# Expert search, segment pacing and gate rows rearranged in a two-layer hybrid decoder trunk

## The reference

```python
mod = silu(c) @ ada_w[l] + ada_b[l]                    # sh_m, sc_m, g_m, sh_f, sc_f, g_f
x = x + g_m * mixer(modulated_norm(x, sh_m, sc_m))
h = modulated_norm(x, sh_f, sc_f)
q = (h @ wq).reshape(128, 8, 2, 128)                   # 8 heads, two halves, chunks of 128 tokens
s = einsum('thcd,hcnd->thcn', q, subkeys)              # 128 scores for each half
sv, si = top_k(s, 16)
cand = sv[..., 0, :, None] + sv[..., 1, None, :]       # 256 candidates
fv, fpos = top_k(cand, 16)                             # 16 experts of each head: 128 a token
coef = softmax(fv) * gelu(u[eidx] . h)
x = x + g_f * sum(coef * v[eidx])
```

## Time and profile before

| | us |
|---|---|
| median of three runs | 1900.18 |
| lowest, highest | 1897.82, 1906.14 |
| the profiled execution's own time | 1903.03 |
| its span in the trace | 1901.2 |
| PE busy | 1616.6 (85%) |
| DVE busy | 1394.7 (73%) |
| ACT busy | 673.4 (35%) |
| POOL busy | 515.2 (27%) |

### The profile page before, as it was taken

How to read it: one execution, slowest core, us unless ns; L and a number is a source line. 1 busy time by engine, 2 the same in 40 slices (tenths; PEclk the granted TensorE clock), 3 DMA queues, 4 the chain that set the end, 5 groups by cost and what they waited for, 6 DMA issues and landing times.

```text
span 1901.2 us, 20926 instructions
## 1 busy us (share of the span) xinstructions
PE 1616.6 (85%) x6868; PEld 1006.0 (53%) x6868; DVE 1394.7 (73%) x3315; ACT 673.4 (35%) x1640; POOL 515.2 (27%) x564
## 2 busy tenths in 40 slices
PE   1767678898999998898999998898999997887776
PEld 1656665554665655564665655554665652332222
DVE  5866598997856758998765748988765759985554
ACT  1313114334732334335632235325632233331112
POOL 2000013222233232222233232222232233343331
PEclk9889788998999999998999999999999998999999
DMA  9982688997799999998999999998899999999996
GB/s 393 422 346 101 242 353 348 367 421 286 283 399 421 422 420 395 363 422 313 321 403 421 421 421 399 370 402 293 287 403 421 421 415 401 416 407 421 421 421 256
DMA packets 96989, 706.08 MB, mean 371 GB/s; under 512 B 10992, under 2 KB 11504, under 8 KB 13296
## 3 DMA queue, kind: packets, MB, share of 16 engines
q0 software_dynamic: 80640, 587.24, 77.1%
q1 hardware_dynamic: 16240, 117.50, 15.1%
HBM read 703.64 MB, written 1.05 MB: 371 GB/s over the span
## 4 chain that ended last, share of the span: by engine, by line
PE 49%; DVE 28%; DMA 16%; ACT 3%; issue 3%; POOL 0%; DVEq 0%; ACTq 0%; POOLq 0%
PE psum L772 26%; DMA ringmem<-in_peer_uv_dram,eidx 11%; DVE ringmem L1435 9%; PE psum L648 5%; PE psum L412 4%; DMA W<-in_w_groups_dram 3%; PE psum L635 2%; DMA ringmem<-in_ada_pairs_dram 2%; PE psum L520 1%; PE psum L508 1%; DVE ringmem L1079 1%; PE psum L518 1%; PE psum L415 1%; DVE coef L1448 1%; ACT diag L1050 1%
## 5 line engine op out<-in xcount | busy, mean ns | idle before, releaser
L772 PE MATMUL psum<-ringmem,diag 128*128 128x512 f32 x2048 | 978.4, 624 | 132.3 <-ACT diag L1050 132.0
L379 POOL DMA_INDIRECT ringmem<-in_peer_uv_dram,eidx x512 | 489.5, 956 | 1131.5 <-PE psum L772 1079.7
L1435 DVE SCALAR_TENSOR_TENSOR ringmem<-ringmem,psum 128x1024 f32<-128x1024 f32 x512 | 612.5, 1220 | 195.3 <-DMA ringmem<-in_peer_uv_dram,eidx 180.1
L772 PEld LDWEIGHTS psum<-ringmem,diag 128*128 128x128 f32 x2048 | 389.1, 199 | 608.1 <-issue 409.1
L1050 ACT ACTIVATE diag<-K,coef 128x128 f32<-128x128 f32 x512 | 176.4, 393 | 225.8 <-DVE coef L1448 225.6
L412 PE MATMUL psum<-hT,W 128*128 128x128 f32 x1344 | 172.3, 287 | 40.9 <-DMA W<-in_w_groups_dram 19.1
L412 PEld LDWEIGHTS psum<-hT,W 128*128 128x128 f32 x1344 | 169.2, 203 | 64.9 <-issue 38.0
L1042 ACT ACTIVATE coef<-dots 128x2 f32<-128x2 f32 x256 | 51.8, 202 | 408.6 <-DVE ringmem L1435 407.7
L1079 DVE SCALAR_TENSOR_TENSOR ringmem<-ringmem,diag 128x1024 f32<-128x1024 f32 x96 | 115.3, 1223 | 20.9 <-DMA ringmem<-in_ada_pairs_dram 18.8
L648 PEld LDWEIGHTS psum<-hT,W 128*128 128x128 f32 x1024 | 123.2, 197 | 12.8 <-issue 7.2
L648 PE MATMUL psum<-hT,W 128*128 128x128 f32 x1024 | 126.0, 281 | 3.1 <-ACT hT L821 3.0
(11 more groups left out here) (243 smaller groups left out, 1629.7 us busy)
## 6 DMA issues: line engine op xcount, KB each, us to landing
ringmem<-in_ada_pairs_dram POOLq DMA_DIRECT2D x48, 1024.0 KB, 19.0
W<-in_w_pieces_dram SPq DMA_DIRECT2D x48, 1024.0 KB, 9.2
W<-in_w_groups_dram SPq DMA_DIRECT2D x24, 1536.0 KB, 11.3
W<-in_w_groups_dram SPq DMA_DIRECT2D x12, 1024.0 KB, 9.6
ringmem<-in_peer_uv_dram,eidx POOLq DMA_INDIRECT x512, 11.7
W<-in_w_groups_dram SPq DMA_DIRECT2D x4, 1040.0 KB, 9.2
attn<-in_subkeys_t_dram SPq DMA_DIRECT2D x4, 1024.0 KB, 9.5
K<-in_consts_dram SPq DMA_DIRECT2D x1, 1546.0 KB, 18.1
```

The lines of the kernel that those rows point to most:

```text
L379: nc.gpsimd.indirect_dma_start(slot(k), None, rows, bass.IndirectOffsetOnAxis(ap=eidx[:, ph % 2, m:m + 1], axis=0)).then_inc(row_landed[q ...
L772: mm = nc.tensor.matmul(acc[:, q], diag[:, k % DIAGS, :], slot(k)[:, D:][:, q], start=(k % SEL == 0), stop=(k % SEL == SEL - 1), skip_grou ...
L1435: ins = v.scalar_tensor_tensor(out=u, in0=u, scalar=1.0, in1=hrep, op0=ALU.mult, op1=ALU.mult, accum_out=dots[:, j:j + 1])
```

## The change

Four things are changed.

The search: from unit 1 on, heads 0 to 3 are searched beside the queries, in segments 61 to 76. In the pass, two heads are searched in ticks 1 to 4, two parts a tick, and heads 6 and 7 in ticks 13 to 20, one part a tick. Unit 0 has only heads 0 and 1 searched in the lead; in its pass heads 4 and 5 stand in ticks 5 to 12.

The pacing: fourteen segments whose work waits on the segment before (1, 2, 43 to 51, 55 to 57) come at most one to a tick; segments start in tick 0 rather than 1; the costs of the last five segments are others. The result: segments 0, 1 and 2 stand in ticks 0, 1 and 2 (before: all in tick 1); segments 5 to 36 each stand about one tick earlier, segment 22 in tick 15 (before: 16), 23 and 24 in 16 (before: 17), 29 in 19 (before: 20), 33 in 23 (before: 24); segments 46 and 47 stand in ticks 37 and 38 (before: both in 38); from segment 48 on they stand where they stood or up to a tick off; 69 to 76 fill ticks 56 to 61.

The gate rows: PE turns the column itself, read as a 128x128 operand with a step of zero, and ACT's scaled identities are gone. Both halves of the expert layer's gate come in segment 75, in banks 6 and 7.

The sum: `add_sum` stands ahead of the segments of tick 0.

```diff
+CHAINED = {1, 2, 43, 44, 45, 46, 47, 48, 49, 50, 51, 55, 56, 57}
...
-    total, done, out = sum(COST), 0, [-1] * TICKS
+    total, done, tick, out = sum(COST), 0, 0, [0] * TICKS
     for n, w in enumerate(COST):
-        tick = 1 + (TICKS - 3) * done // total
+        tick = max((TICKS - 2) * done // total, tick + (n in CHAINED))
...
+def find_ticks(ph):
+    out = [[] for _ in range(TICKS)]
+    for n in range(8):
+        out[1 + n // 2].append((4 - 2 * (ph == 0) + n // 4, n % 4))
+        if ph == 0:
+            out[5 + n].append((4 + n // 4, n % 4))
+        out[13 + n].append((6 + n // 4, n % 4))
+    return out
...
-                def gate_row(nth, src, dst, bank_free):
-                    pe.wait_ge(s["g_diag"], nth + 1)
+                def gate_row(nth, l, section, half, dst, bank_free):
+                    pe.wait_ge(s["mod_ready"], 3 if l else 2)
                     pe.wait_ge(s[bank_free[0]], bank_free[1])
                     for j in range(4):
-                        mm = nc.tensor.matmul(dst[:, j * P:(j + 1) * P], ones[:], src[:, j, :], start=True, stop=True)
-                    mm.then_inc(s["g_out"], 1)
+                        k = 4 * half + j
+                        tr = nc.tensor.transpose(dst[:, j * P:(j + 1) * P],
+                                                 MC[:, l, section, k:k + 1].broadcast_to([P, P]), ident)
+                    tr.then_inc(s["g_out"], 1)
...
-                        if seg in (65, 69):
-                            gate_exp(i, (seg - 65) // 4)
+                        if seg in ((65, 69, 73, 77) if i else (65, 69)):
+                            gate_exp(i, (seg - 62) // 4)
...
-                        if m % 4 == 0 and 2 <= 1 + m // 4 < PH:
-                            gate_exp(ph, 1 + m // 4)
+                        for h, part in FIND[ph][m - 1] if m else []:
+                            if part == 3:
+                                gate_exp(ph, h)
...
-                        elif 61 <= seg <= 68:
+                        elif 61 <= seg <= (76 if i else 68):
                             retrieve(i, (seg - 61) // 4, (seg - 61) % 4)
...
-                        if m < 4 * (PH - 2):
-                            retrieve(ph, 2 + m // 4, m % 4)
-                        beside.upto(PACE[m])
+                        for h, part in FIND[ph][m]:
+                            retrieve(ph, h, part)
                         if m == 0 and ph:
                             add_sum(ph - 1)
+                        beside.upto(PACE[m])
                         coefficients(n)
```

More of the change, by code:

```diff
@@ L127 @@
        "av_out": 1, "av_sb": 1, "uw_out": 1, "u_sb": 1, "w_sb": 1, "sa_out": 2, "sa_sb": 2, "st_out": 2, "st_sb": 2,
-       "y_out": 1, "y_sb": 1, "o_var": 1, "o_sd": 1, "y_var": 1, "y_sd": 1, "mix_ready": 1, "g_diag": 4, "g_out": 4, "g_sb": 4, "wo_out": 4, "wo_taken": 2, "x_mixed": 1,
+       "y_out": 1, "y_sb": 1, "o_var": 1, "o_sd": 1, "y_var": 1, "y_sd": 1, "mix_ready": 1, "g_out": 4, "g_sb": 4, "wo_out": 4, "wo_taken": 2, "x_mixed": 1,
        "q_out": PH, "q_sb": PH, "score_out": PH, "score_sb": PH}
@@ L151, in trunk @@
     PACE, LEAD = pace(), lead_pace()
+    FIND = [find_ticks(ph) for ph in range(PHASES)]
     with ExitStack() as ctx:
@@ L274, in trunk @@
         crow = diag[:].rearrange("p a c -> p (a c)")
-        gdiag = (hT[:, 0:4, :], hm[:, 0:512].rearrange("p (a c) -> p a c", a=4))
         def slot(k):
@@ L710, in mixing @@
                             state_next(0)
-                            gate_row(g_at(i, 0), gdiag[0], bank[4], ("u_sb", at("u_sb", i, 1)))
+                            gate_row(g_at(i, 0), l, G_M, 0, bank[4], ("u_sb", at("u_sb", i, 1)))
                         elif seg == 47:
                             state_sum(1)
-                            gate_row(g_at(i, 1), gdiag[0], bank[4], ("g_sb", g_at(i, 1)))
+                            gate_row(g_at(i, 1), l, G_M, 1, bank[4], ("g_sb", g_at(i, 1)))
                         elif seg == 48:
@@ L738, in mixing @@
                         if i and seg == 75:
-                            gate_row(g_at(i, 2), gdiag[1], bank[6], ("q_sb", at("q_sb", i, 7)))
-                        elif i and seg == 76:
-                            gate_row(g_at(i, 3), gdiag[1], bank[6], ("g_sb", g_at(i, 3)))
-                def gate_row(nth, src, dst, bank_free):
-                    pe.wait_ge(s["g_diag"], nth + 1)
+                            for half in range(2):
+                                gate_row(g_at(i, 2 + half), (i - 1) // NT, G_F, half, bank[6 + half],
+                                         ("q_sb", at("q_sb", i, 7 + half)))
+                def gate_row(nth, l, section, half, dst, bank_free):
+                    pe.wait_ge(s["mod_ready"], 3 if l else 2)
                     pe.wait_ge(s[bank_free[0]], bank_free[1])
                     for j in range(4):
-                        mm = nc.tensor.matmul(dst[:, j * P:(j + 1) * P], ones[:], src[:, j, :], start=True, stop=True)
-                    mm.then_inc(s["g_out"], 1)
+                        k = 4 * half + j
+                        tr = nc.tensor.transpose(dst[:, j * P:(j + 1) * P],
+                                                 MC[:, l, section, k:k + 1].broadcast_to([P, P]), ident)
+                    tr.then_inc(s["g_out"], 1)
                 def last_gate():
[L752 to L755, removed]
+                    yield 75
+                    for half in range(2):
+                        gate_row(g_at(PHASES, half), DEPTH - 1, G_F, half, bank[6 + half],
+                                 ("q_sb", at("q_sb", PHASES, 0)))
                 def place_h(ph):
@@ L791, in gate_exp @@
                     nc.scalar.activation(e, e, exp, accum_out=gsum[:, i % 2, h:h + 1]).then_inc(s["gate_exp"], 1)
[L793 to L797, removed]
                 def gate_copy(nth, half, src):
@@ L973, in mixing @@
                         elif seg == 46:
-                            if i == 0:
-                                act.wait_ge(s["mod_ready"], 2)
-                            gate_diag(l, G_M, 0, gdiag[0])
+                            gate_copy(g_at(i, 0), 0, bank[4][:, :])
                         elif seg == 47:
-                            gate_copy(g_at(i, 0), 0, bank[4][:, :])
-                            gate_diag(l, G_M, 1, gdiag[0])
-                        elif seg == 48:
                             gate_copy(g_at(i, 1), 1, bank[4][:, :])
@@ L1013, in mixing @@
                                                  ACT.Copy).then_inc(s["q_sb"], 1)
-                        if seg in (65, 69):
-                            gate_exp(i, (seg - 65) // 4)
[L1016 to L1020, removed]
+                        if seg in ((65, 69, 73, 77) if i else (65, 69)):
+                            gate_exp(i, (seg - 62) // 4)
+                        if i and seg == 75:
+                            for half in range(2):
+                                gate_copy(g_at(i, 2 + half), half, bank[6 + half][:, :])
                 def squares_last(t):
@@ L1031, in ending @@
                     squares_last(0)
[L1032 to L1037, removed]
+                    yield 76
+                    for half in range(2):
+                        gate_copy(g_at(PHASES, half), half, bank[6 + half][:, :])
                 def activate(n):
```

2 lines of the change are left out of this document (1 added, 1 removed).

## The result

The changed kernel is slightly slower, not 1.6% faster: median 1907.79 us (1904.3 to 1915.25, 12 runs) against 1903.22 us (1897.12 to 1906.14, 12 runs), ratio 1.0033, 95% interval 1.0019 to 1.0048. Its profiled execution took 1906.4 us, with a span of 1904.6 us.

What follows compares the result with a forecast made beforehand. Before tick 39 DVE, then PE, was taken to bound the passes, transfers from there on. -3.2 - 14.4 - 13.7 - 3 + 4.5 - 1 = -30.8 us, 1903.0 to 1872.2, on the median's scale 1870 us; range 1848 to 1893.

Steps and rivals of the forecast that it cites:

- Ticks 0 to 15 of passes 1 and 2: Largest of three limits (DVE 99, PE 107, transfers 103 us) sets the time: -12.1 us in pass 1, -11.4 in pass 2.
- The rival that the weights become late: Ticks 5-15: waits of 2 to 3 us for each of six weight groups, 1885 us; chance 0.16.
- the rival that DVE's limit holds alone: Passes 1 and 2 win 20 us in ticks 0-15, the ends cost nothing, 1849 us; chance 0.17.
- Ticks 17-20: Now ticks 16-19: one chain through the weight load sets 29.7 us; DVE waits longer at segment 29, nothing won.
- Ticks 21-23: Now ticks 20-22: DVE bounds them and only one part 3 of search is left, -4.9 us.
- Ticks 24-38: Now ticks 23-38: PE bounds; one more tick +3.4, splitting segments 46 and 47 -0.8, sum +2.6 us.
- The passes' ends: Passes 0 to 2: two more heads, 20.5 us, hidden in DVE's wait for rows; +1.5 us each, bounds 0 and +10.
- The rival that the lump shows at the ends: Search at the ends isn't covered, 20.5 us lost in each of three passes, 1926 us; chance 0.05.
- Pass 3: Doubled parts in ticks 1-4 are covered by the ring, ticks 5-12 are bare; -3 us, bounds -4 and +5.
- Pass 0: Keeps 24 parts of search, 19 of them in ticks 0-15 (113.8 against 114.7 us); -3.2 us in all.
- Lead: Gate rows: eight matmuls of 1.16 us become eight transposes, -1 us, bounds 0 and -4; nothing charged for PE's clock.
- The rival that the transposes slow PE: A `weigh` slowed from 3.60 to 5.40 us in 12 places, 22 us, giving 1892 us; chance 0.04.

Runs made afterwards that it cites:

- e8: The kernel before with the new pacing alone, and segment 10 also in a tick of its own behind segment 9: ratio 1.0007.
- e9: The changed kernel with heads 4 and 5 searched one part a tick in passes 1 to 3, pass 0 as before, and segment 10 apart: ratio 0.9952.
- e2: The kernel before with the new search alone, old pacing and old gate rows: ratio 0.9969.
- e12: The changed kernel without the second half of the weighted sum, except for the first and last row of each pass: 1842.77 us, ratio 0.9696.
- e5: The kernel before with the new search in passes 1 to 3, but one part a tick in ticks 1 to 8; pass 0 as before: ratio 0.9928.
- e1: The kernel before with only the gate rows made by turning, without scaled identities: ratio 1.0013.
- e7: The kernel before with gate rows made by turning, each transpose issued twice: ratio 0.9981.
- e10: e9 with each transpose of the gate rows issued twice: ratio 0.9912.

## Why the prediction was wrong

The forecast was -30.8 us; the profiled execution moved by +3.4 (+5.1 to its last row product, -1.7 behind it). The step that failed above all is "I take it, though DVE alone would give 20: the three are so close that no one of them is left idle". The steps one by one:

- **Ticks 0 to 15 of passes 1 and 2, "the largest is PE's 107 us": wrong, and the largest error.** 116.5 and 116.0 us were measured; with -12.1 and -11.4 forecast, -2.6 and -2.4 came. The three sums themselves were near: DVE worked 91.6 us for 90.7 forecast, PE 100.1, and the bytes at 421 GB/s make 105 us for 103. Ticks 0 to 4 came near theirs (41.3 for 39), the other eleven took 75 us for 67.6. What failed was to take the largest of three sums for the time: each engine waits in turn for another, DVE 21.8 us in the lines above, PE 16.4. I gave each segment a cost and no hand-over. e8 shows that the pair 9 and 10 is worth 4 us a pass with the old search; with the new search, mending the pair and the doubled parts left 3.4 us at the end of this stretch and 1.0 us at the end of pass 1 (e9), while the wait at segment 18 grew from 6.8 to 9.7 us. e2 says the same from the other side: 11 us less of DVE's work in ticks 0 to 16 won 0.4 us. e12 shows that PE's work was not what held the stretch above its floor. The rival that the weights become late isn't seen: PE waits for none in this stretch. Nor is the rival that DVE's limit holds alone: its sign was a pass 1 of 400 us or less.
- **Ticks 17-20, nothing won: right in its size, not in its reason.** 29.8 us for 29.7. But DVE's wait at segment 29, which was to grow, fell from 6.6 to 2.3 us, and a wait of 5.4 us for ACT's gelu stands in its place.
- **Ticks 21-23, -4.9: right.** 18.8 for 23.8, -5.0.
- **Ticks 24-38, +2.6: the limit right, the size wrong, to the good side.** 91.1 for 91.3, -0.2. PE stays 97% busy with one tick more, but its busy time is 88.6 us, before 89.7. The granted clock rose from 0.98 to 1.00 and a gate row takes some 0.6 us rather than 1.16, neither of which the prediction had.
- **What I left out: ticks 39 to 50**, 75.0 for 71.3 us, +3.7, at 421 GB/s in both. A pass that reaches tick 39 sooner has fetched less, so a stretch at the ceiling takes part of it back: by the rates and lengths in the rows 95.3 MB had come by tick 39, before 96.4, and the difference is 2.6 us of the ceiling. I had made the sum as if all won before tick 39 were kept. By my own measure, (1 - rate/421) of each stretch, what is lost before tick 39 fell from 34.9 to 29.7 us, by 5.2.
- **The passes' ends, +1.5 each: near.** Ticks 51 to 63 changed by -1.1, +0.5 and +2.1 us in passes 0 to 2. In pass 1 the wait for rows fell from 24.4 us to 9.4 (under 8 was forecast): 18 us of search are hidden there. The rate of 414 GB/s in the last seven ticks is under the 415 that was to speak for the rival, and cost 0.7 us. The rival that the lump shows at the ends is refuted; the lump that did show is at the beginning.
- **Pass 3, -3: wrong, +8.0.** "About 30 us for 20 us of rows, which the ring covers" is the step. The 30 us were near (ticks 1 to 4 took 32.5), and the ring was overrated: DVE lost 9.5 us against before in ticks 0 to 4, while POOL stood without a slot. The bare ticks behind bring DVE back to within 0.5 us (tick 24 begins 127.9 us into the pass before, 128.4 in the change), but not the transfers: before, DVE takes ticks 24 to 29 in 23.4 us out of rows that have landed, now it takes 29.8. From tick 30 on both go at 4.97 us a tick, nearly all at the ceiling, where nothing can be made up. e5 shows it: single parts give 316.2 us, -2.3, near the -3 forecast.
- **Pass 0, -3.2, with its end -1.7:** -1.2, which is luck. Ticks 0 to 15 took 116.7 us for 113.8 forecast (they have a doubled start, too, and the pair 9 and 10), ticks 39 to 50 lost 4.8 us that weren't in the sum, and ticks 16 to 38 and the end came out some 7 us better than forecast.
- **Lead, -1 us, and "I charge nothing" for the clock: wrong, +4.5 us** of chain. Two things were wrong. "Eight matmuls of 1.16 us become eight transposes": the 1.16 us are eight records of four matmuls, and they became four records, so PE's work there was halved. And I looked at a place where a turning stands in dense work. In the lead PE works in short bursts, and halving the work of two of them kept it at 1.2 GHz for the 10 us after. e1 and e7 show it from both sides. The rival that the transposes slow PE had the clock in it, but for another reason and in the passes; there a `weigh` behind the gate rows of segments 46 and 47 takes 3.70 us in pass 1, not the 5.4 that were its sign.

The gain of the search is real, 8 us in each of two passes (e2), some 60% of what I forecast, and it lies in ticks 17 to 23. The loss has three causes, each removed by one edit (e5, e8, e7). The measured ratio is 2.0% of the time, 37 us, above the forecast one; the three edits together (e10, 0.9912) win back 1.2%, 23 us. The other 14 us are the first stretches of passes 1 and 2, of which only the wait at segment 18 is named, and what the stretches at the ceiling take back.

## What to carry to other kernels

Where several in-order engines are each about 80% busy or more in a stretch, don't take the largest of their sums for the time: list for each tick which hand-over (DVE to PE and back, DVE to ACT and back) has both its ends in it, and price that. Mend and time again, for the next hand-over may take the time that the first gave back. A lump of work that starves a ring of buffers was made up for here where slower ticks stood behind it (passes 1 and 2), and not where the rest ran at the ceiling (pass 3). Taking work off a matrix engine that runs in bursts can cost more than it saves, if what follows then runs at the lower clock.

## What the runs showed of the hardware that was not expected

In these traces a 128x128 float32 transpose with an operand of step zero takes one matmul record where ones times a 128x128 identity takes two: 1.11 us for four and 2.07 us for eight at the low clock. Issuing these transposes twice (e7) is faster than once (e1), 0.9981 against 1.0013, and even than the kernel before. The lead's chain accounts for 5 us between e1 and e7; why passes 0 and 2 of e7's profile are 1.3 and 4.3 us shorter than before wasn't tried. Of the 4.3 us, 3.1 lie in the single tick 20 of pass 2 (14.8 us before, 11.7 in e7), in which no instruction was changed.
